# A new order of the front steps, one product for both groups' compressed scores, and fillers in three pauses

## The chip, the cores and the metric

The kernel runs as one program on one core of a Trainium2 chip. The metric is the device time of one execution in microseconds. Every number below comes from timed runs or from one profiled execution of the kernel before.

## The reference

One decoder layer over 256 tokens of width 1024, float32 throughout:

```
p = rms_norm(h) @ w_in                      # 3 parts: NSA queries/keys/values, RWKV-7 inputs, gates
o_nsa:  per 2 groups x 4 heads (64 wide): compressed attention over 15 blocks
        k_cmp = rms_norm(silu(blocks(kc) @ ck_w1) @ ck_w2), v_cmp alike without the norm
        + selected-block attention + window attention, each a masked softmax with an ALiBi slope,
        summed with three sigmoid gates
o_rwkv: RWKV-7 over 8 heads of 64: a state of 64x64 per head, group norm, bonus, gate
h = h + concat(o_nsa, o_rwkv) @ w_out
h = h + cross_attention(rms_norm(h), rms_norm(mem))      # 4 heads of 256, 256 memory tokens
h = h + moe(rms_norm(h))                    # top 4 of 32 experts, clamped SwiGLU, 1024 -> 2048 -> 1024
```

With 256 tokens there are at most four selection blocks, so all of them are taken and the selected part is plain causal attention.

## The kernel before

The kernel has two halves. The **front** computes everything up to the router. The **expert loop** then goes over "items", one expert (or the overflow of one) with up to 64 tokens each, and reads 12.6 MB of weights for each item through a ring of six 2 MB pieces in SBUF (`ring`, loaded at L2088). SyncE's queue reloads a piece as soon as TensorE signals `piece_used` for it. The first halves of items 10 to 15 are loaded ahead (L2104) into buffers that the front no longer needs. Item 0's six pieces are loaded during the end of the front, from the moment `rwkv_out` is complete, because the ring's memory serves as the front's scratch until then.

**Order of the front.** After the input projections (TensorE until about 104 us) the work is a list of small steps, `ORDER`. TensorE, VectorE, ScalarE and GpSimd each walk the same list in the same order and execute their own part of each step; each engine is in-order, so a step that waits holds up all that stands behind it on that engine. The steps are:

- `xk j`: key projection for cross-attention, quarter j (32 matmuls of 128x256; a float32 matmul appears as two instructions). ScalarE copies and squares it, GpSimd adds the two squares (L2020, `kx_squares`). `xkn j`: the sum over partitions (L675), `Sqrt` on ScalarE, reciprocal and two multiplies on VectorE. `xv n`: value projection (L684).
- `score u`, `turnp u`, `pv u`: one attention unit (u = 0 to 3 of token tile 0, 4 to 7 of tile 1): scores (L712), `Exp` on ScalarE, normalising on VectorE and GpSimd (L2016), transposes (L733), product with the values (L748, L753).
- `cmp`, `cmpout`, `cmpsc`, `turnc`: compressed keys and values. `cmp` (L474) needs its own weight slot, job `cmp` of the list `LATE`. `cmpout` (L482 to L492) goes TensorE, ScalarE, VectorE, TensorE, ScalarE, VectorE in turn and ends with `kcmpT`. `cmpsc` (L696) computes the compressed scores, with 64 rows of the array for each of the two groups and 15 columns each.
- `tok`, `parts`, `g3`, `inv 0..14`, `akv`, `qt`, `z`, `chunk 0..3`, `y`, `ymean`, `yvar`: the RWKV part. `inv s` (L551, 32 small products each) is a chain that inverts 64x64 triangular matrices; ScalarE copies some results out of PSUM, VectorE the others. `yvar 1` ends in `rwkv_out`.

PSUM results rotate over seven banks in the order of the list (`tile`), so a step also waits until the result seven tiles back has been taken. Behind the list stand the output projection (L773), whose first 32 of 128 instructions need only the attention part and whose rest waits for `rwkv_out`; the cross-attention with its own list `CROSS` (L822 to L860); its output projection with the router (L325, L874 to L914); and `gather` (L922), which collects the tokens of the first items.

**ScalarE's function tables.** The function of an ACTIVATE must be in the table set that is loaded. A set is loaded by name with `preload_act_table_set`; where none is named, the compiler places a load in front of the ACTIVATE that needs one. The code names the set that holds both `Ln` and `Exp` (`LOGEXP`) at L1623, L1666 and last in `cmpout` (L1710); from there to L1889 no set is named. Every inverse root in that stretch is the pair

```
link(f(dst, src, ACT.Ln, scale=scale, bias=...))
link(f(dst, dst, ACT.Exp, scale=-0.5), name)
```

which is used in `cmpout`, `yvar 0` and `yvar 1`, `token_rs` (twice) and the four `norm` steps of `CROSS`; `xkn` uses `ACT.Sqrt`.

**Item 0.** `hidden_bias` (L944) adds the first-layer bias as a small product; item 0 does two of them, then 32 instructions of `hidden` (L964) over the pieces 0 and 1, then the other half. VectorE's `hot` column selects the bias.

`keep_busy(n)` issues n products of 128x128 whose result nobody reads.

Of the kernel before, what the change touches and what calls it, by code (L numbers as in the profile page):

```python
# [53 lines left out]
LATE = [('xk_w', 0), ('xk_w', 1), ('xk_w', 2), ('xk_w', 3), ('xv_w', 0), ('cmp', 0), ('xv_w', 1), ('xv_w', 2),  # L54
# [41 lines left out]
def build(nc, a, out):  # L96

    ctx = ExitStack()
    with ctx:
# [32 lines left out]
        kcmpT = sb("kcmpT", 16)  # L132
# [136 lines left out]
        def matrix(q, tt, p):  # L269
# [4 lines left out]
        ORDER = [('xk', 0), ('score', 0), ('tok', 0), ('cmpin',), ('xkn', 0), ('xk', 1), ('score', 1), ('parts', 0),  # L274
                 ('xkn', 1), ('xk', 2), ('parts', 1), ('g3',), ('xkn', 2), ('xk', 3), ('xkn', 3), ('inv', 0),
                 ('inv', 1), ('xv', 0), ('inv', 2), ('cmp',), ('cmpout',), ('tok', 3), ('cmpsc',), ('inv', 3),
                 ('turnc', 0), ('xv', 1), ('turnp', 0), ('turnp', 1), ('score', 2), ('akv',), ('inv', 4), ('inv', 5),
                 ('pv', 0), ('score', 3), ('inv', 6), ('inv', 7), ('xv', 2), ('pv', 1), ('turnp', 2), ('score', 4),
                 ('inv', 8), ('xv', 3), ('turnp', 3), ('pv', 2), ('inv', 9), ('inv', 10), ('score', 5), ('tok', 1),
                 ('pv', 3), ('inv', 11), ('xv', 4), ('inv', 12), ('turnc', 1), ('turnp', 4), ('turnp', 5),  # L280
                 ('inv', 13), ('pv', 4), ('score', 6), ('inv', 14), ('score', 7), ('tok', 2), ('pv', 5), ('qt',),
                 ('z',), ('turnp', 6), ('turnp', 7), ('chunk', 0), ('pv', 6), ('chunk', 1), ('y', 0), ('pv', 7),
                 ('chunk', 2), ('xv', 5), ('chunk', 3), ('ymean', 0), ('y', 1), ('yvar', 0), ('xv', 6), ('ymean', 1),
                 ('xv', 7), ('yvar', 1)]

        CROSS = [('project', 0), ('project', 1), ('norm', 0), ('score', 0), ('score', 1), ('norm', 1),
                 ('project', 2), ('turn', 0), ('turn', 1), ('score', 2), ('score', 3), ('norm', 2), ('project', 3),
                 ('score', 4), ('score', 5), ('pv', 0), ('turn', 2), ('turn', 3), ('turn', 4), ('norm', 3),
# [14 lines left out]
        def _(pe):  # L303
# [174 lines left out]
            def cmpout_step():  # L478
                pe.wait_ge(sem("cmp_hidden"), 1)
# [177 lines left out]
            def yvar_step(tt):  # L657
                pe.wait_ge(sem("y_squared"), tt + 1)
                t = tile("yvar", tt, freed=("y_rs", tt + 1))
                pe.matmul(t, blk64[:, :], SQ, start=True, stop=True).then_inc(sem("tile_ready"), 1)  # L660
# [27 lines left out]
            def cmpsc_step():  # L688
                pe.wait_ge(sem("queries_normed"), 2)
                pe.wait_ge(sem("kcmp"), 1)  # L690
                for tt in range(TT):
                    both = [tile("cmpsc", tt, g, freed=("cmp_scores", 2 * tt + g + 1)) for g in range(NSA_G)]
                    for i in range(4):
                        for g in range(NSA_G):
                            r = slice(64 * g, 64 * g + 64)
                            mm = pe.matmul(both[g][:, i * 16:i * 16 + NCMP], qT[r, i, tt * P:(tt + 1) * P],  # L696
                                           kcmpT[r, 0:NCMP], start=True, stop=True)
                            if i == 3:
                                mm.then_inc(sem("tile_ready"), 1)
# [147 lines left out]
            def xturn(n):  # L847
                pe.wait_ge(sem("xprobs"), n + 1)
# [92 lines left out]
            def hidden_bias(g):  # L941

                n, half, r = g // 2, g % 2, slice(NE * g, NE * g + NE)
                pe.matmul(psum[64 * half:64 * half + 64, 4 + n, :], hot[r, :], bias1[r, :], start=True, stop=False)  # L944
# [1292 lines left out]
```

## Time and profile before

| | us |
|---|---|
| median of 3 runs | 1283.32 (1283.27 to 1283.56) |
| the profiled execution's own time | 1287.24 |
| its span in the profile | 1285.5 |
| TensorE busy | 1228.3 |
| TensorE weight loads busy | 620.0 |
| VectorE busy | 361.1 |
| ScalarE busy | 195.4 |
| GpSimd busy | 58.7 |
| bytes moved | 442.61 MB, mean 344 GB/s |

Busy time is an average over stages with different limits; the stages have to be read apart. In the profile L12 is line 12 of the kernel, PE is TensorE, PEld its weight load, DVE VectorE, ACT ScalarE, POOL GpSimd, and SP the queue of SyncE that issues the weight loads. All of ScalarE's activations carry the line of the helper (L1607).

### The profile page before, as it was taken

What the parts mean: (1) busy time and instruction counts of PE and PEld (TensorE: products, weight loads), DVE (VectorE), ACT (ScalarE), POOL (GpSimd) and SP (SyncE); (2) the same over time, 40 slices, a digit from 0 to 9 for tenths busy, and PEclk for the clock granted to TensorE, in tenths of its full rate; (3) what the DMA queues carried; (4) which work ended last, traced back from release to release, by engine and by line L of the source; (5) the groups of instructions that cost most, each with busy time, mean ns of one, the idle gap of its engine ahead of it and who ended that gap; (6) DMA issues with size and microseconds to landing.
All of it is one profiled execution on the core that took longest, in us unless ns stands there. A gap on an engine that the chain in (4) does not pass through costs nothing.

```text
span 1285.5 us, 19154 instructions
## 1 busy us (share of the span) xinstructions
PE 1228.3 (96%) x7762; PEld 620.0 (48%) x7762; DVE 361.1 (28%) x850; ACT 195.4 (15%) x437; POOL 58.7 (5%) x110
## 2 busy tenths in 40 slices
PE   9999898999999999999899999999999998989898
PEld 8887777788773343323234333434423232323332
DVE  4467754322235221212122121212212121212111
ACT  2333335312210000000000000000000000000001
POOL 6210001100010000000000000000000000000000
PEclk9999989999999999999999999999999999999999
DMA  7342110197379999999999999999999999999997
GB/s 261 136 150 104 67 68 35 36 369 317 122 316 400 428 428 428 429 429 428 429 427 429 421 395 424 428 428 428 428 429 429 429 428 429 428 429 428 429 427 303
DMA packets 36343, 442.61 MB, mean 344 GB/s; under 512 B 4032, under 2 KB 4160, under 8 KB 6592
## 3 DMA queue, kind: packets, MB, share of 16 engines
q1 hardware_dynamic: 35424, 440.24, 82.0%
q10 hardware_dynamic: 864, 1.57, 0.4%
q8 instruction: 43, 0.70, 0.2%
q14 instruction: 12, 0.10, 0.0%
HBM read 440.75 MB, written 1.05 MB: 344 GB/s over the span
## 4 chain that ended last, share of the span: by engine, by line
PE 63%; DMA 30%; DVE 3%; ACT 2%; issue 1%; POOL 0%; ACTq 0%; SPq 0%; DVEq 0%
DMA sb_ring<-in_mlp_w 29%; PE ps L964 23%; PE ps L993 9%; PE ps L325 8%; PE ps L922 3%; PE ps L932 2%; PE ps L822 2%; PE ps L773 2%; PE ps L684 2%; PE ps L944 1%; PE ps L551 1%; PE ps L979 1%; PE ps L338 1%; ACT sb_qx L1607 1%; PE ps L426 1%
## 5 line engine op out<-in xcount | busy, mean ns | idle before, releaser
L964 PE MATMUL ps<-sb_ring,sb_xv 128*64 128x512 f32 x1960 | 439.7, 596 | 29.7 <-DMA sb_ring<-in_mlp_w 28.7
L964 PEld LDWEIGHTS ps<-sb_ring,sb_xv 128*64 128x64 f32 x1960 | 133.5, 137 | 311.8 <-issue 252.3
L993 PE MATMUL ps<-sb_ring,sb_xv 128*64 128x512 f32 x1024 | 228.6, 596 | 0.0
L1567 DVE TENSOR_SCALAR sb_early<-ps 128x256 f32<-128x256 f32 x64 | 27.2, 425 | 646.9 <-PE ps L964 646.9
L993 PEld LDWEIGHTS ps<-sb_ring,sb_xv 128*64 128x64 f32 x1024 | 71.7, 137 | 133.1 <-issue 131.0
L1607 ACT ACTIVATE sb_early<-sb_early 128x256 f32<-128x256 f32 (+2 forms) x69 | 28.2, 409 | 512.8 <-DVE sb_early L1567 507.7
L1607 ACT ACTIVATE sb_early<-ps 128x512 f32<-128x512 f32 (+2 forms) x39 | 21.1, 543 | 280.2 <-PE ps L993 266.0
L932 PE MATMUL ps<-sb_early 64*128 64x512 f32 x248 | 61.6, 615 | 0.0
L922 PE MATMUL ps<-sb_early,sb_hnT 128*128 128x128 f32 x512 | 59.8, 275 | 0.0
L922 PEld LDWEIGHTS ps<-sb_early,sb_hnT 128*128 128x128 f32 x512 | 58.4, 192 | 0.0
L325 PE MATMUL ps<-sb_hnT,sb_wsl 128*128 128x256 f32 x256 | 56.1, 379 | 0.0
L325 PEld LDWEIGHTS ps<-sb_hnT,sb_wsl 128*128 128x128 f32 x256 | 48.6, 190 | 7.1 <-issue 0.5
L1542 DVE TENSOR_TENSOR sb_xv<-ps,sb_xv 128x512 f32<-128x512 f32 x32 | 22.1, 691 | 55.1 <-PE ps L922 55.1
L979 PEld LDWEIGHTS ps<-sb_ident,sb_xv 128*128 128x128 f32 x128 | 12.9, 141 | 50.9 <-issue 26.0
L944 PE MATMUL ps<-sb_early,sb_hot 32*64 32x512 f32 x256 | 35.9, 613 | 0.0
L1607 ACT ACTIVATE sb_xv<-ps 128x256 f32<-128x256 f32 x64 | 24.0, 375 | 50.0 <-PE ps L979 50.0
L932 PEld LDWEIGHTS ps<-sb_early 64*128 64x128 f32 x248 | 21.3, 186 | 19.8 <-issue 19.8
L684 PE MATMUL ps<-sb_wsl,sb_ox 128*128 128x256 f32 x128 | 30.8, 395 | 0.0
L325 PE MATMUL ps<-sb_qx,sb_wsl 128*128 128x256 f32 x128 | 28.4, 381 | 0.7 <-ACT sb_qx L1607 0.7
L325 PE MATMUL ps<-sb_ox,sb_wsl 128*128 128x256 f32 x128 | 28.4, 380 | 0.7 <-DVE sb_qx L1111 0.7
L979 PE MATMUL ps<-sb_ident,sb_xv 128*128 128x128 f32 x128 | 28.1, 301 | 0.5 <-DVE sb_xv L1574 0.5
L822 PE MATMUL ps<-sb_hnT,sb_wsl 128*128 128x256 f32 x128 | 28.5, 381 | 0.0
(374 smaller groups left out, 1043.1 us busy)
## 6 DMA issues: line engine op xcount, KB each, us to landing
sb_ring<-in_mlp_w SPq DMA_DIRECT2D x183, 2048.0 KB, 20.7
sb_wsl<-in_w_front SPq DMA_DIRECT2D x31, 1024.0 KB, 4.8
sb_ring<-in_mlp_w SPq DMA_DIRECT2D x5, 1024.0 KB, 21.7
sb_wsl<-in_mlp_w SPq DMA_DIRECT2D x3, 1024.0 KB, 8.9
sb_spare<-in_mlp_w SPq DMA_DIRECT2D x2, 1024.0 KB, 9.6
sb_ring<-in_mlp_w SPq DMA_DIRECT2D x4, 512.0 KB, 13.8
sb_wsl<-in_w_values SPq DMA_DIRECT2D x1, 1120.0 KB, 5.0
sb_wsl<-in_w_front ACTq DMA_DIRECT2D x4, 256.0 KB, 7.3
```

Source lines behind the costliest of these rows:

```text
L325: mm = pe.matmul(t[:, g * T:(g + 1) * T], w[:, k, g * P:(g + 1) * P], act[:, k, :], start=k == 0, stop=k == KD - 1)
L684: mm = pe.matmul(t[:, 0:T], memT[:, k, tt * P:(tt + 1) * P], wjob(J_XV[j])[:, k, :], start=k == 0, stop=k == KD - 1)
L773: mm = pe.matmul(t[:, g * T:(g + 1) * T], w[:, k, g * P:(g + 1) * P], mixT[:, k, :], start=k == 0 and g == 0, stop=k == KD - 1, skip_group ...
L822: mm = pe.matmul(t[:, g * T:(g + 1) * T], w[:, k, g * P:(g + 1) * P], hnT[:, k, :], start=k == 0, stop=k == KD - 1)
L922: mm = pe.matmul(psum[:, 4 + k // 4, k % 4 * PAIR:(k % 4 + 1) * PAIR], h[:, tt, k * P:(k + 1) * P], sel[:, tt, :], start=tt == 0, stop=tt ...
L932: mm = pe.matmul(psum[:, 2 * tt + o2, :], selgT[par][r, tt, :], yb[r, :], start=False, stop=False, skip_group_check=True)
L944: pe.matmul(psum[64 * half:64 * half + 64, 4 + n, :], hot[r, :], bias1[r, :], start=True, stop=False)
L964: mm = pe.matmul(psum[64 * half:64 * half + 64, 4 + n, :], xgT[:, k, SLOTS * par:SLOTS * par + SLOTS], w[:, at + 512 * half:at + 512 * hal ...
L979: mm = pe.transpose(psum[:, 6, m * P:(m + 1) * P], actv[:, m * P:(m + 1) * P], ident[:, :])
L993: mm = pe.matmul(psum[64 * o2:64 * o2 + 64, 7, :], actT[:, 2 * n + m, 64 * q:64 * q + 64], ring[:, at + 512 * o2:at + 512 * o2 + 512], sta ...
L1567: dve.tensor_scalar(gl, psum[:, 4 + n, 0:256], 7.0, None, ALU.min).then_inc(sem("glu"), 1)
L1607: return act.activation(o, x, func, **kw)
```

## The change

The edits: a new `ORDER`; a new `CROSS`; job `cmp` one place earlier in `LATE`; the compressed scores of both groups in one product of 128 rows by 32 columns, from a `kcmpT` that holds each group in its own rows and zeros elsewhere (eight products instead of sixteen, one PSUM tile and one VectorE add for each token tile instead of two); fillers of four products in `cmpout`, in `yvar 1` and ahead of the first `turn` of `CROSS`; the addition of the two squares in `xk` on VectorE instead of GpSimd; one small memset more on GpSimd; and item 0's bias products behind the weights' products of each half instead of ahead of them.

```
@@ -51,7 +51,7 @@
-LATE = [('xk_w', 0), ('xk_w', 1), ('xk_w', 2), ('xk_w', 3), ('xv_w', 0), ('cmp', 0), ('xv_w', 1), ('xv_w', 2),
+LATE = [('xk_w', 0), ('xk_w', 1), ('xk_w', 2), ('xk_w', 3), ('cmp', 0), ('xv_w', 0), ('xv_w', 1), ('xv_w', 2),
@@ -129,7 +129,7 @@
-        kcmpT = sb("kcmpT", 16)
+        kcmpT = sb("kcmpT", NSA_G, 16)
@@ -271,21 +271,21 @@
-        ORDER = [('xk', 0), ('score', 0), ('tok', 0), ('cmpin',), ('xkn', 0), ('xk', 1), ('score', 1), ('parts', 0),
-                 ('xkn', 1), ('xk', 2), ('parts', 1), ('g3',), ('xkn', 2), ('xk', 3), ('xkn', 3), ('inv', 0),
-                 ('inv', 1), ('xv', 0), ('inv', 2), ('cmp',), ('cmpout',), ('tok', 3), ('cmpsc',), ('inv', 3),
-                 ('turnc', 0), ('xv', 1), ('turnp', 0), ('turnp', 1), ('score', 2), ('akv',), ('inv', 4), ('inv', 5),
-                 ('pv', 0), ('score', 3), ('inv', 6), ('inv', 7), ('xv', 2), ('pv', 1), ('turnp', 2), ('score', 4),
-                 ('inv', 8), ('xv', 3), ('turnp', 3), ('pv', 2), ('inv', 9), ('inv', 10), ('score', 5), ('tok', 1),
-                 ('pv', 3), ('inv', 11), ('xv', 4), ('inv', 12), ('turnc', 1), ('turnp', 4), ('turnp', 5),
-                 ('inv', 13), ('pv', 4), ('score', 6), ('inv', 14), ('score', 7), ('tok', 2), ('pv', 5), ('qt',),
-                 ('z',), ('turnp', 6), ('turnp', 7), ('chunk', 0), ('pv', 6), ('chunk', 1), ('y', 0), ('pv', 7),
-                 ('chunk', 2), ('xv', 5), ('chunk', 3), ('ymean', 0), ('y', 1), ('yvar', 0), ('xv', 6), ('ymean', 1),
-                 ('xv', 7), ('yvar', 1)]
+        ORDER = [('xk', 0), ('tok', 0), ('score', 0), ('cmpin',), ('xkn', 0), ('xk', 1), ('score', 1), ('parts', 0),
+                 ('xkn', 1), ('xk', 2), ('parts', 1), ('g3',), ('xkn', 2), ('xk', 3), ('inv', 0), ('cmp',),
+                 ('cmpout',), ('inv', 1), ('tok', 3), ('cmpsc',), ('xkn', 3), ('xv', 0), ('inv', 2), ('akv',),
+                 ('xv', 1), ('xv', 2), ('turnc', 0), ('inv', 3), ('turnp', 0), ('turnp', 1), ('score', 2),
+                 ('inv', 4), ('pv', 0), ('pv', 1), ('inv', 5), ('score', 3), ('inv', 6), ('xv', 3), ('inv', 7),
+                 ('turnp', 2), ('inv', 8), ('turnp', 3), ('score', 4), ('score', 5), ('inv', 9), ('xv', 4),
+                 ('pv', 2), ('inv', 10), ('tok', 1), ('pv', 3), ('inv', 11), ('turnc', 1), ('turnp', 4),
+                 ('turnp', 5), ('pv', 4), ('score', 6), ('inv', 12), ('inv', 13), ('tok', 2), ('pv', 5), ('inv', 14),
+                 ('score', 7), ('xv', 5), ('z',), ('turnp', 6), ('turnp', 7), ('qt',), ('chunk', 0), ('chunk', 1),
+                 ('pv', 6), ('chunk', 2), ('y', 0), ('chunk', 3), ('pv', 7), ('ymean', 0), ('y', 1), ('yvar', 0),
+                 ('xv', 6), ('ymean', 1), ('xv', 7), ('yvar', 1)]
...
-                 ('project', 2), ('turn', 0), ('turn', 1), ('score', 2), ('score', 3), ('norm', 2), ('project', 3),
-                 ('score', 4), ('score', 5), ('pv', 0), ('turn', 2), ('turn', 3), ('turn', 4), ('norm', 3),
+                 ('project', 2), ('score', 2), ('score', 3), ('turn', 0), ('turn', 1), ('turn', 2), ('turn', 3),
+                 ('norm', 2), ('score', 4), ('project', 3), ('pv', 0), ('turn', 4), ('norm', 3), ('score', 5),
@@ -476,6 +476,7 @@
             def cmpout_step():
+                keep_busy(4)
@@ -655,6 +656,8 @@
             def yvar_step(tt):
+                if tt:
+                    keep_busy(4)
@@ -687,16 +690,13 @@
             def cmpsc_step():
...
-                pe.wait_ge(sem("kcmp"), 1)
+                pe.wait_ge(sem("kcmp"), NSA_G)
...
-                    both = [tile("cmpsc", tt, g, freed=("cmp_scores", 2 * tt + g + 1)) for g in range(NSA_G)]
+                    t = tile("cmpsc", tt, freed=("cmp_scores", tt + 1))
...
-                        for g in range(NSA_G):
-                            r = slice(64 * g, 64 * g + 64)
-                            mm = pe.matmul(both[g][:, i * 16:i * 16 + NCMP], qT[r, i, tt * P:(tt + 1) * P],
-                                           kcmpT[r, 0:NCMP], start=True, stop=True)
-                            if i == 3:
-                                mm.then_inc(sem("tile_ready"), 1)
+                        mm = pe.matmul(t[:, i * 32:i * 32 + 32], qT[:, i, tt * P:(tt + 1) * P],
+                                       kcmpT[:, :, :].rearrange("p g c -> p (g c)"), start=True, stop=True)
+                    mm.then_inc(sem("tile_ready"), 1)
...
             def score_step(u):
@@ -845,6 +845,8 @@
             def xturn(n):
+                if n == 0:
+                    keep_busy(4)
@@ -938,10 +940,11 @@
-            def hidden_bias(g):
+            def hidden_bias(g, last=False):
...
-                pe.matmul(psum[64 * half:64 * half + 64, 4 + n, :], hot[r, :], bias1[r, :], start=True, stop=False)
+                return pe.matmul(psum[64 * half:64 * half + 64, 4 + n, :], hot[r, :], bias1[r, :],
+                                 start=not last, stop=last)
...
             def hidden(i, par, n, stage, ahead, last):
@@ -963,7 +966,12 @@
-                                       w[:, at + 512 * half:at + 512 * half + 512], start=False, stop=k == KD - 1)
+                                       w[:, at + 512 * half:at + 512 * half + 512],
+                                       start=stage == 0 and k == 0, stop=stage > 0 and k == KD - 1)
+                    if stage == 0 and k == KD - 1:
+                        pe.wait_ge(sem("hot"), 1)
+                        for g in (2 * n, 2 * n + 1):
+                            mm = hidden_bias(g, last=True)
@@ -1001,10 +1009,11 @@
-                pe.wait_ge(sem("hot"), i + 1)
...
-                for g in range(2 if first else 4):
-                    hidden_bias(g)
+                if not first:
+                    pe.wait_ge(sem("hot"), i + 1)
+                    for g in range(4):
+                        hidden_bias(g)
@@ -1019,9 +1028,6 @@
-                if first:
-                    for g in range(2, 4):
-                        hidden_bias(g)
@@ -1246,8 +1252,11 @@
-                link(stt(kcmpT[:, 0:NCMP], psum[:, b, 0:NCMP], vec("k_cmp_norm_g"), crs[:, 0:NCMP],
-                         ALU.mult, ALU.mult), "kcmp")
+                dve.wait_ge(sem("kcmp_cleared"), 1)
+                for g in range(NSA_G):
+                    r = slice(64 * g, 64 * g + 64)
+                    link(stt(kcmpT[r, g, 0:NCMP], psum[r, b, 0:NCMP], vec("k_cmp_norm_g")[r, :], crs[r, 0:NCMP],
+                             ALU.mult, ALU.mult), "kcmp")
...
             def parts_step(tt):
@@ -1353,11 +1362,10 @@
-                    for g in range(NSA_G):
-                        b = ready(dve, "cmpsc", tt, g)
-                        part = sc_c[:, tt, 4 * g:4 * g + 4, 0:NCMP]
-                        link(dve.tensor_tensor(part, view(psum[:, b, :], 0, 4, 16)[:, :, 0:NCMP], part, ALU.add),
-                             "cmp_scores")
+                    b = ready(dve, "cmpsc", tt)
+                    scores = psum[:, b, 0:128].rearrange("p (j g c) -> p g j c", j=4, g=NSA_G)[:, :, :, 0:NCMP]
+                    part = sc_c[:, tt, :, :].rearrange("p (g j) c -> p g j c", g=NSA_G)[:, :, :, 0:NCMP]
+                    link(dve.tensor_tensor(part, scores, part, ALU.add), "cmp_scores")
@@ -1368,6 +1376,10 @@
+
+            def xk_step(j):
+                dve.wait_ge(sem("kx_squared"), j + 1)
+                link(dve.tensor_tensor(xsq[:, 0, :], xsq[:, 0, :], xsq[:, 1, :], ALU.add), "kx_squares")
...
             def score_step(u):
@@ -1395,8 +1407,8 @@
-                     "ymean": ymean_step, "yvar": yvar_step, "xkn": xkn_step, "cmpsc": cmpsc_step, "score": score_step,
-                     "turnp": turnp_step}
+                     "ymean": ymean_step, "yvar": yvar_step, "xk": xk_step, "xkn": xkn_step, "cmpsc": cmpsc_step,
+                     "score": score_step, "turnp": turnp_step}
@@ -1980,6 +1992,7 @@
+            link(pool.memset(kcmpT[:, :, :], 0.0), "kcmp_cleared")
@@ -2015,15 +2028,9 @@
-            def xk_step(j):
-                pool.wait_ge(sem("kx_squared"), j + 1)
-                pool.tensor_tensor(xsq[:, 0, :], xsq[:, 0, :], xsq[:, 1, :], ALU.add).then_inc(sem("kx_squares"), 1)
-
...
-                if step == "xk":
-                    xk_step(*args)
...
             def add_squares(which):
...
```

## Rows read from the trace of the kernel before

**Rows 1.** The page's slices: GB/s in 40 slices of 32.1 us.
```profile
GB/s 261 136 150 104 67 68 35 36 369 317 122 316 400 428 428 428 429 429 428 429 427 429 421 395 424 428 428 428 428 429 429 429 428 429 428 429 428 429 427 303
```
**Rows 2.** Windows: bounds, length, PE, PEld, DVE, ACT, POOL busy, PEclk, DMA share, GB/s.
```profile
100.00:262.00 162.00, 145.57 (x2358) 122.00 (x2357) 89.53 (x171) 69.38 (x162) 15.01 (x12) 0.94 0.19 65
...
388.00:390.00 2.00, 2.00 (x12) 0.73 (x13) 1.86 (x6) 0.80 (x2) 0.00 (x0) 1.00 0.90 254
...
430.00:440.00 10.00, 10.00 (x52) 3.12 (x50) 0.39 (x2) 0.60 (x1) 0.00 (x0) 1.00 1.00 425
```
**Rows 3.** Timeline of TensorE, 104 to 262 us: start, length, instructions, [idle before, releaser].
```profile
112.41 0.72 PE L712 MATMUL ps<-sb_hn 64*128 64x128 f32 x8 [0.81 <-issue]
...
145.43 0.96 PE L675 MATMUL ps<-sb_early 128*128 128x256 f32 x2 [2.37 <-POOL sb_early L2020]
...
157.96 0.29 PE L482 MATMUL ps<-sb_h1T,sb_smalls 64*64 64x15 f32 x4 [1.55 <-DVE sb_h1T L1243]
...
161.07 3.60 PE L696 MATMUL ps<-sb_kcmpT,sb_hn 64*128 64x15 f32 x32 [0.47 <-issue]
...
167.00 4.93 PE L684 MATMUL ps<-sb_wsl,sb_ox 128*128 128x256 f32 x16
...
179.36 1.16 PE L551 MATMUL ps<-sb_spare,sb_ring 64*64 64x64 f32 x45 [2.63 <-issue]
...
185.29 3.72 PE L684 MATMUL ps<-sb_wsl,sb_ox 128*128 128x256 f32 x16
...
209.81 1.38 PE L551 MATMUL ps<-sb_early,sb_spare 64*64 64x64 f32 x64 [2.14 <-ACT sb_spare L1607]
...
224.55 1.16 PE L566 MATMUL ps<-sb_ring 64*64 64x64 f32 x64 [2.04 <-ACT sb_ring L1607]
```
**Rows 4.** Windows in which the clock was low (columns as in Rows 2).
```profile
160.00:170.00 10.00, 9.54 (x109) 8.44 (x108) 6.16 (x25) 3.95 (x10) 0.50 (x1) 0.52 0.01 2
...
212.00:214.00 2.00, 2.00 (x12) 2.00 (x11) 0.00 (x0) 1.87 (x4) 0.00 (x0) 0.50 0.03 8
```
**Rows 5.** Timeline of POOL: the sum of squares of `xk 0`.
```profile
113.09 0.73 POOL L2020 TENSOR_TENSOR sb_early<-sb_early 128x256 f32<-128x256 f32 x1 [44.88 <-ACT sb_early L1607]
```
**Rows 6.** Timeline of DVE: what stands ahead of it, and a 128x256 addition.
```profile
112.34 1.42 DVE L1220 TENSOR_TENSOR sb_ring<-ps,sb_ring 128x512 f32<-128x512 f32 x2
...
236.46 0.42 DVE L1308 TENSOR_TENSOR sb_ring<-ps,sb_ring 128x256 f32<-128x256 f32 x1 [1.30 <-PE ps L622]
```
**Rows 7.** Groups by line, ACT: automatic table loads (busy, mean ns, idle before).
```profile
L1607 ACT ACT_TABLE_LOAD x4 | 5.1, 1283 | 6.7 <-DVE sb_st L1384 6.6
```
**Rows 8.** Timeline of ACT: a table load, and the pair of `yvar 0`.
```profile
120.28 1.28 ACT L1607 ACT_TABLE_LOAD   x1
121.57 0.47 ACT L1607 ACTIVATE sb_early<-ps,sb_eps_col 128x256 f32<-128x256 f32 x1
...
250.90 0.69 ACT L1607 ACTIVATE sb_ring<-ps,sb_eps_col 128x512 f32<-128x512 f32 x1 [0.46 <-PE ps L660]
251.62 0.63 ACT L1607 ACTIVATE sb_ring<-sb_ring 128x512 f32<-128x512 f32 x1
```
**Rows 9.** Timeline of DVE in `ymean 1`.
```profile
256.06 0.69 DVE L1322 TENSOR_TENSOR sb_ring<-sb_ring,ps 128x512 f32<-128x512 f32 x1
```
**Rows 10.** Timelines of PE and SP: output projection, and first ring load.
```profile
259.26 27.79 PE L773 MATMUL ps<-sb_mixT,sb_wsl 128*128 128x256 f32 x128
...
264.68 0.33 SPq L2088 DMA_DIRECT2D sb_ring<-in_mlp_w  x1
```
**Rows 11.** Timeline of PE in the cross-attention: its longest waits.
```profile
313.19 0.44 PE L851 MATMUL ps<-sb_ident,sb_hn 128*128 128x128 f32 x2 [1.44 <-DVE sb_hn L1434]
...
338.02 14.08 PE L325 MATMUL ps<-sb_qx,sb_wsl 128*128 128x256 f32 x64 [0.75 <-ACT sb_qx L1607]
```
**Rows 12.** Timelines of DVE and PE: router, and item 0's bias.
```profile
371.67 0.54 DVE L1111 SCALAR_TENSOR_TENSOR sb_early<-ps,sb_st,sb_smalls 128x32 f32<-128x32 f32 x2 [3.45 <-ACT sb_st L1607]
...
379.83 1.07 PE L944 MATMUL ps<-sb_early,sb_hot 32*64 32x512 f32 x4
```

## The prediction

> **What bounds the kernel now.** I read the slices first, then windows, then the timeline of each stage. From the middle of the trace on, the slices stand at 421 to 429 GB/s almost without a break [rows 1], and a window inside the expert loop has the DMA engines busy for 1.00 of it [rows 2]. So the second part is bound by the weight stream: 12.6 MB an item, about 29 us, while TensorE has slack there. The stream runs from the moment item 0 gives its first pieces back. The front before it isn't bound by DMA: it moves little [rows 1], and TensorE's queue is the chain. So a microsecond won or lost before `gather` is one won or lost at the end, and one inside the loop is worth nothing. The changed steps lie between 104 and 380 us.
>
> In the list (100 to 262 us) TensorE is busy for 145.57 of 162 us, so 16.4 us are idle, at a mean granted clock of 0.94 [rows 2]. That mean means 0.06 x 162 = 9.7 us of full-speed time not granted; some of it fell into idle time, so I take 8.5 as what work was stretched by. The idle time is in a few holes: 0.81, 2.37, 1.55, 0.47, 2.63, 2.14 and 2.04 us are the main ones [rows 3]. The low level (0.50 in a window, 1.2 GHz) shows soon after several of the holes [rows 4]; the same value projection takes 4.93 us at 167 us and 3.72 at 185 [rows 3]. The hole of 2.04 us wasn't followed by a fall.
>
> **The list, step by step.** I walked the new order with the durations of the old rows, each engine in order, and noted where TensorE waits.
> - Gone: the idle time but 0.5 us that lies ahead of the list, 15.9, and the 8.5 of the clock. `xkn 3` with its wait of 2.37 now stands behind `cmpsc`, when its operand is long ready; `tok 0` covers the 0.81.
> - `cmpsc`: 32 instructions took 3.60 us at half clock [rows 3, 4], 112 ns each, 56 at full; 16 fewer are worth 0.9. VectorE loses two small adds, no one waits for them. The second small write of `kcmpT` costs VectorE 0.2 and the memset is early on GpSimd, whose queue has nothing due: nothing.
> - The square sum: 0.73 us on GpSimd [rows 5] becomes about 0.42 on VectorE [rows 6]. But in `xk 0` VectorE still has the two bonus products until 113.8 [rows 6] and then a memset, so `xkn 0` can start at 114.7, while TensorE arrives at 113.2: a new hole of 1.5. Behind the waiting VectorE stand the score steps; later ones lose under 0.5 each, bounds 0 and 1.5.
> - `cmpout` comes right behind `inv 0` and `cmp`. ScalarE has the inversion's two copies and its table load (1.28) ahead of the exponential, so the wait is about 2.4 instead of 1.55: filler 1.1 and 1.3 idle. So the filler itself costs no time here.
> - `turnp 0` and `1` wait for VectorE and GpSimd: 0.95. `inv 8` 0.75, `turnp 5` 0.85, `turnp 7` 0.45, the chunk steps 2.0 together.
> - `inv 14` needs copies that on ScalarE stand behind the exponentials of `score 6`: 1.7.
> - Together 1.5 + 2.4 + 0.95 + 0.75 + 0.85 + 0.45 + 2.0 + 1.7 = 10.6 of new waits.
> - The hole of 2.63 with no releaser [rows 3] lies in a burst of weights: TensorE had nothing to issue. The new order puts slow value projections into most bursts, but not all; bounds 0 and 2.6, I take 1.3. The clock may still fall after one or two holes: bounds 0 and 8.5 (as before), I take 2.0.
> Sum: -15.9 - 8.5 - 0.9 + 10.6 + 1.3 + 2.0 = -11.4, with -17 and -4 as ends.
> `LATE` moves one load ahead of another; both slots are free over 10 us before their use: nothing.
>
> **What the list takes with it: tables.** Before, all of `xkn` (`Sqrt`) came ahead of `cmpout`, which names the set with `Ln` and `Exp`; from there on no load stands in the trace until the loop. Now `xkn 3` comes behind `cmpout`. It brings in the set of `Sqrt`, `score 2` another for `Exp`, and no one names the joint set again. An automatic load for `Exp` need not bring `Ln`. I take it that it doesn't: then each `Ln`, `Exp` pair behind it costs two loads: two in `yvar 0`, two in `yvar 1`, two in each `token_rs`, two in each of four `norm`, so 18 with the two of `xkn 3` and `score 2`. A load takes 1.283 us [rows 7], and the activation behind it follows at once [rows 8]: 2.57 a pair.
> - `yvar`: the pair's 2.57 moves y_rs from 252.3 to 254.8, VectorE's steps behind it, the subtraction of `ymean 1` (256.06 [rows 9]) and so the square that `yvar 1` waits for. TensorE starts the output projection 1.8 later than its work allows (the filler of 1.1 lies in that wait). The second pair delays `rwkv_out`, which let the ring loads go at 264.68 [rows 10], by another 2.57, and the first 32 of 128 instructions cover 7.0 us [rows 10]: 1.0 more. Together +2.8; bounds 1.1 (the filler alone) and 5.1 (both pairs bare). The ring loads wait with it; their weights are due 5 us and more later, so that is hidden.
> - `CROSS`: the wait of 1.44 at the first `turn` [rows 11] gets two scores ahead of it. But the norms' pairs hold ScalarE and, in order behind them, VectorE's copy of project 2 and later scores. I get a wait of 2.0 at `turn 0` (1.1 of it filler), 0.4 at `norm 3` and 2.0 at `turn 5`, against 1.44 + 0.64 + 0.2 before: `xout`, at 338.02 [rows 11], moves by +1.8; bounds -1.0 (nothing added) and +6.
> - Router: VectorE waits 3.45 us and starts at 371.67 on ScalarE's inverse root [rows 12]. All that follows (choice, places, selection, `gather`) hangs on it: +2.5; bounds 0 and 2.6. TensorE then idles 2.5 us ahead of `gather`; the clock may fall there: +1.4, bounds 0 and 4.8 (the ten microseconds at 160 had a mean clock of 0.52 [rows 4]).
>
> The row shows 1.28 us for a load and 0.01 until the next activation [rows 8]. The Trainium skill, ScalarE: Activation LUTs, section What ACT_TABLE_LOAD costs, has a drain of 1.38 us beside the load, 2.66 us a switch. By that rule the pairs would cost 5.3 each. The trace disagrees: ScalarE's load at 120.28 ends at 121.56 and its `Sqrt` starts at 121.57. The same page (section Table sets) says that `Ln` then `Exp` needs one load when the joint set is used, which is what the first rival is about.
>
> **Item 0's bias.** Two products of 1.07 us together move from ahead of `hidden` to behind it [rows 12]. The first quarter of piece 0 comes free 1.07 earlier, but piece 1 is given back behind the bias, at the same time as before, and the stream was already starved just then (254 GB/s at 388 [rows 2]). So 0; bounds -1.1 and 0.
>
> **Sum.** -11.4 + 2.8 + 1.8 + 2.5 + 1.4 = -2.9 us. Made against the profiled execution, 1287.24 us (span 1285.5, 1.7 around it), this is 1284.3 there; that execution is 3.9 above the median, and the difference carries over: 1283.32 - 2.9 = 1280.4.
>
> **Rivals.**
> - *The tables don't come*, since the automatic load brings the joint set. Then -11.4, +1.1 for the filler in `yvar 1` (no wait there for it to fill), -1.0 in `CROSS`: -11.3, 1272.0. For it: four automatic loads in the trace are all we see, and none was followed by an `Ln`. Against: the code names the joint set by hand each time. 5 in 100.
> - *The clock stays low.* Place: from `cmp` to `turnc`, with few columns a product, and in the same way after later holes. If thin products rather than holes bring the fall, the 8.5 us aren't won, and a filler of 1.1 changes nothing. -2.9 + 8.5 - 2.0 = +3.6: 1286.9. It decides the sign once over 5 of the 8.5 stay. For it: from 160 to 170 us TensorE was busy nearly all the time at 0.52 [rows 4]. Against: the holes ahead of each fall. 20 in 100.
> - *My walk is too dark*: half of the new waits aren't there, and no fall: -2.9 - 5.3 - 1.3 = -9.5: 1273.8. 15 in 100.
> - *A switch costs more than its row*: 1.38 more for each of some nine loads on the path, +12.4: 1292.8. This is the rule of the skill's page named above. 3 in 100.
>
> **How the numbers follow.** The forecast has 57 in 100, with its own range 1276.5 to 1284.5. A difference under 0.2% (2.6 us) can't be told from none. The forecast lies just beyond that: 27 faster, 22 same, 8 slower. With the rivals: faster 27 + 5 + 15 = 47; same 22 + 6 = 28; slower 8 + 14 + 3 = 25. The range 1273.5 to 1287.5 takes in the low clock and the lighter walk and leaves out the tables' absence and the dearer switch.
>
> **What would show it.** ScalarE's table loads 28 instead of 10, with a pair of them around every `Ln`; `cmpsc` in 16 instructions at about 1 us; the window 100 to 250 at a clock above 0.97; the output projection starting near 250 us instead of 259.26 and waiting once for `rwkv_out`; `xout` 6 to 7 us earlier than 338; VectorE's router step waiting about 6 us instead of 3.45. Wrong would be: no load behind `score 2`; a clock still at 0.94; or TensorE waits in the list over 15 us.

## The result, and the profile after

The changed kernel took 1291.01 us (median of 12 runs, 1285.31 to 1293.86), the kernel before 1283.64 beside it (12 runs, 1282.79 to 1285.08): ratio 1.0053, 95% interval 1.0043 to 1.0064. The forecast was 1280.4, faster, range 1273.5 to 1287.5: wrong in sign, and the time lies outside the range. Executions of one kernel differ by several microseconds here, so below a kernel stands for its ratio, and 0.001 is 1.3 us.

The profiled execution of after has a span of 1289.8 us, against 1285.5. The tables came as forecast. The groups of ScalarE by line, after (columns as in [rows 7]):
```profile
L1619 ACT ACT_TABLE_LOAD x22 | 28.2, 1283 | 9.5 <-DVE sb_st L1396 6.6
```
22 automatic loads instead of 4, 28 in all instead of 10. ScalarE's timeline in `yvar 0`:
```profile
244.55 1.28 ACT L1619 ACT_TABLE_LOAD   x1 [0.44 <-PE ps L663]
245.84 0.69 ACT L1619 ACTIVATE sb_ring<-ps,sb_eps_col 128x512 f32<-128x512 f32 x1
246.54 1.28 ACT L1619 ACT_TABLE_LOAD   x1
247.84 0.63 ACT L1619 ACTIVATE sb_ring<-sb_ring 128x512 f32<-128x512 f32 x1
```
Each `Ln` and each `Exp` gets its own load, with 0.01 us between load and activation, as in [rows 8]: the dearer switch of the last rival isn't there. Against this, the Trainium skill, ScalarE: Activation LUTs, section Table sets, counts one load for `Ln` then `Exp`: that holds here only after the joint set was named by hand.

The waits of the walk came too. TensorE's timeline, after:
```profile
148.03 0.29 PE L483 MATMUL ps<-sb_h1T,sb_smalls 64*64 64x15 f32 x4 [1.29 <-DVE sb_h1T L1249]
...
152.71 1.87 PE L697 MATMUL ps<-sb_kcmpT,sb_hn 128*128 128x32 f32 x16
...
210.19 1.70 PE L552 MATMUL ps<-sb_ring 64*64 64x64 f32 x64 [2.17 <-ACT sb_ring L1619]
...
227.05 0.30 PE L622 MATMUL ps<-sb_ring 64*64 64x64 f32 x2 [0.70 <-DVE sb_ring L1311]
...
254.70 7.07 PE L773 MATMUL ps<-sb_mixT,sb_wsl 128*128 128x256 f32 x32
262.70 3.50 PE L773 MATMUL ps<-sb_mixT,sb_wsl 128*128 128x256 f32 x15 [0.93 <-DVE sb_mixT L1343]
...
312.09 1.61 PE L853 MATMUL ps<-sb_ident,sb_hn 128*128 128x128 f32 x6 [1.10 <-DVE sb_hn L1446]
...
332.00 1.63 PE L853 MATMUL ps<-sb_ident,sb_hn 128*128 128x128 f32 x6 [2.10 <-DVE sb_hn L1446]
333.45 5.33 PE L862 MATMUL ps<-sb_hn,sb_vx 128*128 128x256 f32 x16
...
339.53 2.64 PE L325 MATMUL ps<-sb_qx,sb_wsl 128*128 128x256 f32 x11 [0.75 <-ACT sb_qx L1619]
...
377.77 0.66 PE L911 MATMUL ps<-sb_early,sb_before 128*128 128x64 f32 x2 [2.63 <-DVE sb_early L1480]
...
381.32 5.33 PE L924 MATMUL ps<-sb_early,sb_hnT 128*128 128x128 f32 x32
```
Forecast 1.3 idle at `cmpout` and 2.0, 2.0 in `CROSS`; here 1.29, 1.10 behind a filler of 1.05, and 2.10. `rwkv_out` is waited for once (0.93). At the router (timeline of VectorE, after) the forecast was "about 6":
```profile
375.74 0.54 DVE L1117 SCALAR_TENSOR_TENSOR sb_early<-ps,sb_st,sb_smalls 128x32 f32<-128x32 f32 x2 [6.01 <-ACT sb_st L1619]
```

What didn't come is the clock. Below, a hole is idle time of TensorE in its stream of work, and a fall is a stretch in which the granted clock stands at 0.50 (1.2 GHz). Windows, after (columns as in [rows 2]):
```profile
100.00:262.00 162.00, 149.66 (x2375) 125.94 (x2374) 95.54 (x179) 77.07 (x168) 11.73 (x8) 0.95 0.21 73
...
150.00:152.00 2.00, 2.00 (x49) 1.88 (x42) 1.13 (x3) 0.65 (x3) 0.00 (x0) 0.50 0.06 16
210.00:214.00 4.00, 3.81 (x73) 2.87 (x74) 0.00 (x0) 2.53 (x5) 0.00 (x0) 0.57 0.01 4
227.00:237.00 10.00, 9.26 (x167) 8.59 (x170) 2.90 (x7) 0.00 (x0) 0.00 (x0) 0.53 0.01 2
333.00:337.00 4.00, 3.85 (x12) 3.12 (x12) 1.18 (x7) 1.09 (x3) 0.00 (x0) 0.57 0.01 2
377.00:381.00 4.00, 3.23 (x15) 3.23 (x16) 2.82 (x15) 2.62 (x4) 0.00 (x0) 0.61 0.25 104
381.00:385.00 4.00, 4.00 (x22) 4.00 (x22) 1.43 (x9) 0.00 (x0) 0.00 (x0) 0.54 0.00 0
```
0.95 in the list, against 0.94 [rows 2]; and the clock now falls in `CROSS` and at `gather`, where before it stood at 1.00. The last 16 instructions of `CROSS` take 5.33 us there. In e1_joint, the run below without the added loads, they take 3.72 (TensorE's timeline):
```profile
327.84 3.72 PE L862 MATMUL ps<-sb_hn,sb_vx 128*128 128x256 f32 x16
```
By two-microsecond windows, the full-speed time not granted (length times 1 - PEclk) is 10.2 us up to 264 and none up to 400 in the profile of before; after 8.5 and 5.1. Of the signs that the prediction named, three failed: a clock above 0.97, an output projection near 250 us, and an `xout` 6 to 7 us earlier (it is 1.5 later).

The way through the front by starts of the same products, in us:

| | before | after | e1_joint | h1_best_fill |
|---|---|---|---|---|
| output projection | 259.26 | 254.70 | 253.29 | 248.58 |
| first product of `CROSS`'s queries | 286.89 | 283.52 | 280.92 | 276.20 |
| `xout` | 338.02 | 339.53 | 332.31 | 327.59 |
| `gather` | 376.17 | 381.32 | 370.04 | 365.32 |
| first expert product | 380.84 | 386.58 | 373.80 | 369.09 |
| span | 1285.5 | 1289.8 | 1278.2 | 1273.4 |

### The profile page after: what moved, and what is told of

Same layout as the page of the kernel before. It is cut to its first block, busy times and chain, and to the rows that moved or that the text cites. A ratio compares the mean times of both kernels' runs of the same rounds, so it can differ in the third digit from the quotient of the medians.

```text
span 1289.8 us, 19188 instructions
## 1 busy us (share of the span) xinstructions
PE 1234.1 (96%) x7770; PEld 626.2 (49%) x7770; DVE 364.9 (28%) x853; ACT 218.5 (17%) x455; POOL 55.3 (4%) x107
## 3 DMA queue, kind: packets, MB, share of 16 engines
HBM read 440.75 MB, written 1.05 MB: 343 GB/s over the span
## 4 chain that ended last, share of the span: by engine, by line
PE 45%; DMA 27%; DVE 1%; ACT 1%; issue 0%; SPq 0%; ACTq 0%; DVEq 0%
DMA sb_ring<-in_mlp_w 27%; PE ps L967 24%; PE ps L1001 10%; PE ps L924 3%; PE ps L934 3%; PE ps L325 2%; PE ps L946 1%; PE ps L987 1%; PE ps L1021 1%; PE ps L862 0%; ACT L1619 0%; PE ps L1072 0%; PE ps L876 0%; PE ps L349 0%; DVE sb_early L1117 0%
## 5 line engine op out<-in xcount | busy, mean ns | idle before, releaser
L325 PE MATMUL ps<-sb_hnT,sb_wsl 128*128 128x256 f32 x256 | 56.1, 379 | 0.0
L773 PE MATMUL ps<-sb_mixT,sb_wsl 128*128 128x256 f32 x128 | 28.1, 380 | 0.9 <-DVE sb_mixT L1343 0.9
```

Of the source, the lines that this page charges most:

```text
L325: mm = pe.matmul(t[:, g * T:(g + 1) * T], w[:, k, g * P:(g + 1) * P], act[:, k, :], start=k == 0, stop=k == KD - 1)
L773: mm = pe.matmul(t[:, g * T:(g + 1) * T], w[:, k, g * P:(g + 1) * P], mixT[:, k, :], start=k == 0 and g == 0, stop=k == KD - 1, skip_group ...
```

## The experiments

The theories: (A) the loss is the table loads, and one load of the joint set by hand removes them; (B) what the order gains is less than the sum said, because idle holes and with them the clock's falls stay.

**e1_joint**: one line in the kernel after.
```
 def xkn_step(j):    # ScalarE
     ...
     root(xrs[:, :], psum[:, b, 0:T], "kx_rs")
+    if j == 3:
+        act.preload_act_table_set(LOGEXP)
```


> The changed kernel with one line more: ScalarE names the set that holds Ln and Exp again right behind the Sqrt of xkn 3. Table theory: the 16 later loads go (28 become 12), and with them 1.7 to 2.8 us before the output projection, 3 us in CROSS, 2.5 us of wait at the router and the clock fall behind that wait (1.7), so about 9 us less than the changed kernel: near 1282 us, gather near 372 us in the trace. Rival, the clock in the list is all of it and the loads are hidden: no change, 1291 us, gather near 381.

1279.27 us (7 runs), ratio 0.9958 (0.9944 to 0.9973). Against after, 0.0095 or 12.2 us: theory A holds. Of the 18 added loads one automatic load and the one by hand are left (ScalarE's groups by line, e1_joint):
```profile
L1619 ACT ACT_TABLE_LOAD x5 | 6.4, 1283 | 5.3 <-DVE sb_st L1396 5.2
```
The loads cost more than the 8.4 of my terms: 1.7 in the list (2.8 less the filler's 1.1, which the change pays without loads too), 1.8 + 1.0 in `CROSS`, 3.9 at the router. The change without them gains 5.4, not the 11.3 of the first rival.

**e2_before_lost**: the reverse, in the kernel before.
```
 def cmpout_step():  # ScalarE, at its end
+    act.preload_act_table_set("sqrt_and_others")
```


> The kernel before, with nothing but the joint set lost: behind cmpout ScalarE names the set of Sqrt, so that each Ln, Exp pair later brings its two loads, in the old order and without fillers. Table theory: the loads alone make the kernel before 7 to 9 us slower, 1291 to 1293 us, with the router's choice waiting 6 us instead of 3.45 and a fall of the clock ahead of gather. Rival, the new order's clock and waits are what costs: under 2 us slower, 1284 to 1285.5 us.

1300.62 us (4 runs), ratio 1.0118 (1.0101 to 1.0136). ScalarE's group by line, e2_before_lost:
```profile
L1607 ACT ACT_TABLE_LOAD x21 | 26.9, 1283 | 9.8 <-DVE sb_st L1384 6.6
```
That is 21 automatic loads instead of 4 and one more by hand, 28 in all as in after. The loads alone slow the old order by 15 us, about twice the 7 to 9 expected; the new one isn't needed for it. Its profile has the two falls of after, in `CROSS` and ahead of `gather`; the rest of the excess is open.

**e3_joint_oldcross** and **e4_joint_oldbias**: e1_joint with one more part undone in each.
```
-CROSS = [...]   # order of after, filler at turn 0
+CROSS = [...]   # order of before, no filler
```


> As e1_joint, with the old CROSS list and without the filler ahead of its first turn. If the new CROSS is worth the 1.0 us that I gave it without loads, this is 1 us above e1_joint (1283). Rival: the two lists are alike within 0.5 us once no load stands in them.

0.9958 (0.9944 to 0.9972), 12 runs: without loads the new `CROSS` order is worth nothing measurable; from its first product to `xout` it takes 51.39 us in e1_joint, 51.13 before, and 52.77 in this run, with a fall behind its holes. My -1.0 for it failed.
```
 for g in ...:
-    hidden_bias(g, last=True)   # behind the products
+    hidden_bias(g)              # ahead of them
```


> As e1_joint, with item 0's bias products ahead of the weights' products as before. My account: piece 1 comes free at the same time either way, so no difference (0 to 0.5 us). Rival: the first ring load starts 1.07 us earlier with the new place, and all behind it: this one 1.1 us above e1_joint.

0.9971 (0.9958 to 0.9984), 11 runs, 1280.6: 1.3 above e1_joint, with overlapping intervals. The forecast for the new place was 0, with -1.1 as a bound; which of them holds stays open.

**f1_joint_nofill**: e1_joint without the three fillers.
```
-keep_busy(4)        # in cmpout
-if tt:
-    keep_busy(4)    # in yvar 1
-if n == 0:
-    keep_busy(4)    # at CROSS's first turn
```


> e1_joint without the three fillers of the change (cmpout, yvar 1, first turn of CROSS). If the fillers only sit in waits, the time stays at 1279.3 us; by my account the one in yvar 1 has no wait behind it once the loads are gone and the one in CROSS is longer than its wait, so this is up to 1.5 us faster. Rival, the fillers hold the clock: the low stretches in the list grow from 5 to 8.5 us of lost full-speed time toward 10, and the time goes up by 2 us or more.

0.9958 (0.9946 to 0.9970), 6 runs: the change's fillers neither cost nor bring anything measurable in time. The full-speed time not granted is 9.8 us in the mean of these runs against 7.7 in e1_joint; with 6 and 7 runs that may be chance.

**f2_joint_poolxk**: e1_joint with the square sum on GpSimd.
```
-dve.tensor_tensor(xsq[:, 0, :], xsq[:, 0, :], xsq[:, 1, :], ALU.add)
+pool.tensor_tensor(xsq[:, 0, :], xsq[:, 0, :], xsq[:, 1, :], ALU.add)
```


> e1_joint with the addition of the two squares on GpSimd again. My account: the hole of 1.5 us ahead of xkn 0 (VectorE is still at the bonus products) goes, the other three additions are as early on either engine: 0.8 to 1.5 us less, 1278. Rival: VectorE's faster addition pays at the later three steps, and this is not faster.

0.9949 (0.9933 to 0.9966), 8 runs. TensorE's wait for `xkn 0` is 0.75 instead of the 1.54 of after; the gain of 1.2 is no more than the interval.

**f3_after_routerfill**: the kernel after, loads left in, the router's hole filled.
```
-keep_busy(6)
+keep_busy(16)
```


> The changed kernel, loads and all, with ten more filler products in the router's wait (16 instead of 6 ahead of the wait for the choice), so that TensorE isn't idle for 2.6 us there. If the idle time is what brings the clock down ahead of gather, gather takes 3.7 instead of 5.3 us and the small products ahead of it half, 3 us less in all: 1288. Rival, the fall comes from something else: gather still at 5.3 us, 1291.

1.0032 (1.0020 to 1.0045), 5 runs, 1289.58. TensorE's timeline there:
```profile
380.80 0.43 PE L911 MATMUL ps<-sb_early,sb_before 128*128 128x64 f32 x2 [0.40 <-DVE sb_early L1480]
...
382.84 3.84 PE L924 MATMUL ps<-sb_early,sb_hnT 128*128 128x128 f32 x32
```
The wait for VectorE stays, the hole in TensorE's work goes (2.63 to 0.40), and `gather` runs at full clock: 3.84 us instead of 5.33. So the fall hung on the hole. In time it is 0.0021 or 2.7 us less than after, near the 3 expected, though the intervals touch.

**f4_joint_fills**: e1_joint with fillers in holes that are left.
```
-keep_busy(4)        # cmpout
+keep_busy(9)
+keep_busy(8, both[0][:, 0:P])       # inv 14, ahead of its wait
+keep_busy(2, t[:, 256:256 + P])     # each chunk, ahead of its wait
```


> e1_joint with more fillers: nine products instead of four in cmpout, eight ahead of the wait of inv 14, two in each chunk step's wait. If idle holes bring the clock down, the list keeps the full clock (loss under 2 us instead of 5 to 8.5) and the time falls by 3 us or more, to 1276, with the runs closer together. Rival, thin products of 64 rows bring it down: the falls stay and the time is 1279 to 1281.

0.9948 (0.9935 to 0.9961), 5 runs, all within 1276.42 to 1278.61. The clock is full (windows, f4_joint_fills):
```profile
104.00:400.00 296.00, 283.86 (x3116) 226.58 (x3116) 144.96 (x328) 98.25 (x227) 21.71 (x18) 1.00 0.47 183
```
The falls are gone, as expected, though holes of up to 1.63 us are left, and 8.5 us of lost full-speed time are back. The 3 us of time are not: against e1_joint it is 0.0010 or 1.3 us, inside the intervals, and the output projection starts only 2.7 earlier (250.60).

**g1_best**: f4's fillers, f2's square sum, without the fillers of `yvar 1` and of `CROSS`.
```
-if tt:
-    keep_busy(4)    # yvar 1
-if n == 0:
-    keep_busy(4)    # CROSS's first turn
```


> The kernel after, with one load of the table that holds Ln and Exp behind the root of group 3, the square sum back on GpSimd, fillers ahead of the waits of cmpout (9), inv 14 (8) and the chunks (2 each), and without the fillers of yvar 1 and of CROSS's first turn. Theory (the rest of the list's gain is lost where TensorE stands idle and its clock then falls): no stretch below 0.9 of the clock between 104 and 400 us in the profile, mean clock about 1.00, time 1275 to 1277, at or a little below the 1276.8 and 1277.9 of the two versions that had one of the two edits. Rival (falls come by chance, whatever stands in the holes): a clock of 0.990 to 0.995 as elsewhere, time 1278 to 1280. Second rival (the two dropped fillers hid something): a new low stretch right behind yvar 1 or behind CROSS's first turn and 1.7 us more.

0.9932 (0.9918 to 0.9945), 5 runs, 1275.75. One fall is left up to 400 us, and it is where the dropped filler was (TensorE's timeline, then windows, of g1_best):
```profile
304.00 2.20 PE L854 MATMUL ps<-sb_ident,sb_hn 128*128 128x128 f32 x8 [1.37 <-DVE sb_hn L1443]
```
```profile
306.00:310.00 4.00, 4.00 (x15) 3.37 (x14) 1.07 (x5) 1.43 (x5) 0.00 (x0) 0.57 0.00 0
```

**h1_best_fill**: g1_best with that filler back.
```
+if n == 0:
+    keep_busy(4)
```


> The fastest version so far (g1_best: one hand-set load, square sum on GpSimd, fillers ahead of cmpout, inv 14 and the chunks) with the 4 filler matmuls (1.1 us) ahead of CROSS's first turn put back, where TensorE waits 1.4 us at 304 us and the clock then fell for 3.4 us. Theory (the falls start behind idle holes): no stretch at the low clock between 104 and 400 us, mean clock 0.999 or 1.000, time 1274.5 to 1275.5 against 1275.75. Rival (the fall comes all the same): a stretch at 306 to 310 us again and a clock of 0.998.

0.9934 (0.9922 to 0.9947), 1275.2 us, five runs within 0.8. The hole of 1.37 is now 0.47 behind the filler, and the clock is 1.00 from 104 to 400 us (TensorE's timeline, then the window):
```profile
304.15 0.44 PE L856 MATMUL ps<-sb_ident,sb_hn 128*128 128x128 f32 x2 [0.47 <-DVE sb_hn L1445]
```
```profile
104.00:400.00 296.00, 284.86 (x3118) 226.42 (x3118) 144.17 (x324) 98.25 (x227) 25.10 (x22) 1.00 0.48 185
```
It beats both kernels: 0.66% under before, and by the two ratios 1.2% under after. In time it can't be told from g1_best.

**g2_before_fills**: only fillers, in the kernel before.
```
+keep_busy(6)                        # cmpout
+keep_busy(8, both[0][:, 0:P])       # inv 12, and the same in qt
+keep_busy(9, t[:, 256:256 + P])     # xkn 3
```


> The kernel before with nothing but fillers in its own holes: 9 ahead of group 3's squares, 6 in cmpout, 8 ahead of the inversion step at 179 us and 8 ahead of the qt product at 210 us. Theory: the falls of the clock at 145, 159, 179 and 210 us, which cost 10.2 us of full-speed time in the profile of before, go with the holes, in part paid back since the waits behind them are then met by an engine that comes early: 1276 to 1280, so 4 to 8 us below before. Rival (the falls cost little, since TensorE at half speed is waited for by nothing that matters there): 1282 to 1285. That would say why the change's eight removed microseconds of idle time and its better clock brought less than the sum.

0.9974 (0.9964 to 0.9985), 8 runs: 3.3 us for four fillers, less than the 4 to 8 expected. The falls at 145 and 210 us are gone; one is left in the compressed scores, behind a hole of 1.00 without a filler, and one behind the hole with no releaser, where no filler was tried either. A third is new, in `CROSS` from 310.7 to 314.1, behind holes that brought none in before (TensorE's timeline, then windows):
```profile
159.48 2.72 PE L704 MATMUL ps<-sb_kcmpT,sb_hn 64*128 64x15 f32 x32 [1.00 <-issue]
...
176.27 0.38 PE L556 MATMUL ps<-sb_ring 64*64 64x64 f32 x9 [2.40 <-issue]
```
```profile
160.00:168.00 8.00, 8.00 (x102) 7.20 (x102) 5.79 (x23) 2.48 (x6) 0.91 (x1) 0.57 0.01 2
177.00:181.00 4.00, 4.00 (x96) 3.37 (x91) 2.98 (x6) 1.19 (x2) 0.00 (x0) 0.57 0.03 8
```

**g3_before_cmpsc**: the merged product alone, with the writes and the memset it needs, in the kernel before.
```
-for g in range(NSA_G):   # 64 rows, 15 columns each
-    mm = pe.matmul(both[g][...], qT[r, i, ...], kcmpT[r, 0:NCMP], ...)
+mm = pe.matmul(t[:, i * 32:i * 32 + 32], qT[:, i, ...], kcmpT[...], ...)
```


> The kernel before with one part of the change alone: both groups' compressed scores in one product (16 instead of 32 matmuls, three more small VectorE results). Forecast of that term: -0.9 us. Expected 1282 to 1284, which with the clock's own spread is no difference; 1280 or less would say that the term was worth more (the 32 products ran at half speed), 1286 or more that the wait for the two cleared and written halves of the key tile costs more than the products saved.

1.0008 (0.9999 to 1.0017), 11 runs. TensorE's timeline:
```profile
159.70 3.60 PE L694 MATMUL ps<-sb_kcmpT,sb_hn 128*128 128x32 f32 x16 [0.84 <-issue]
```
16 instructions of 128 rows and 32 columns take 3.60 us at the low clock, exactly what 32 of 64 rows took [rows 3]; and the wait ahead is 0.84 instead of 0.47.

**g4_xkn3_early**: the kernel after with `xkn 3` moved, nothing preloaded.
```
-('inv', 0), ('cmp',), ... ('cmpsc',), ('xkn', 3), ('xv', 0),
+('inv', 0), ('xkn', 3), ('cmp',), ... ('cmpsc',), ('xv', 0),
```


> The kernel after with one name moved: xkn 3 ahead of cmp, so that the root of group 3 is taken before the exponential of the compressed attention and the table of the roots is not called back behind it. Nothing is preloaded. Theory (the 18 added table loads are the loss, and what sets them off is the root behind the exponential): at most 12 table loads, time 1278 to 1282, as with the preload (1279.3), less up to 2 us of TensorE's wait for group 3's squares, which then stands open earlier in the list. Rival (the loads are set off by something else, such as the yvar pairs): 28 loads or so and 1288 to 1292.

0.9985 (0.9968 to 1.0001), 7 runs, 1281.34. ScalarE's group by line, g4_xkn3_early:
```profile
L1619 ACT ACT_TABLE_LOAD x4 | 5.1, 1283 | 5.2 <-DVE sb_st L1396 5.2
```
So it is the root behind the exponential that sets the loads off. The runs lie from 1279.6 (mean clock 0.996) to 1287.87 (0.988); the profiled one is the slowest, with this (windows):
```profile
146.00:166.00 20.00, 19.57 (x182) 17.52 (x183) 13.03 (x32) 5.75 (x15) 0.00 (x0) 0.51 0.19 72
```

**h2_joint_cross** and **h3_joint_router**: the kernel after with the joint set named only ahead of `CROSS`, or only ahead of the router.
```
+act.preload_act_table_set(LOGEXP)
 block_squares("mixed")      # h2; "crossed" in h3
```


> The kernel after with one load by hand of the table that holds Ln and Exp ahead of the first block squares of CROSS: the six loads of the list stay (xkn 3, score 2, two pairs of yvar), those of CROSS and the router go. The forecast's terms for these: 2.8 for CROSS and 3.9 for the router with the clock, so 1291.0 - 6.7 = 1284.3. From the two profiles (CROSS 4.6, router 5.6, of it given back in the loop about 1.4): 1291.0 - 8.8 = 1282.2. The list's share is what is left above 1279.3.

> The kernel after with one load by hand ahead of the last block squares, behind CROSS: the loads of the list and of CROSS stay, the two of the router's inverse root go. Forecast's term: 2.5 for the wait of VectorE and 1.4 for the fall of the clock behind TensorE's idle time, so 1287.1; from the profiles (2.6 + 1.5 + what the loop gives back) 1286.9 to 1288.3. VectorE's wait there 3.45 instead of 6.0, gather 3.7 us long instead of 5.3. f3_after_routerfill, which kept the loads and filled only the hole, gave 1.4 of it.

h2 0.9979 (0.9967 to 0.9992), h3 1.0019 (1.0007 to 1.0030), 12 runs each. By differences of ratios, each uncertain by some 2 us, the loads cost 4.4 at the router (after less h3), 5.1 in `CROSS` (h3 less h2) and 2.7 in the list (h2 less e1).

## Why the prediction was wrong

| term | forecast | measured, from |
|---|---|---|
| the change, no loads | -11.3 | -5.4 (e1) |
| loads in the list | +1.7 | +2.7 (h2 - e1) |
| loads in `CROSS` | +2.8 | +5.1 (h3 - h2) |
| loads in the router, with its fall | +3.9 | +4.4 (after - h3) |
| sum | -2.9 | +6.8 |

Of the 9.7 us between the sums, 5.9 lie in the first line and 3.8 in the loads.

**The step that failed** is the clock term of the list: "the 8.5 of the clock" under "Gone", with "after one or two holes ... I take 2.0", so -6.5. What the runs showed: before has a mean clock of 0.9917 over the 80 runs beside the experiments (10.7 us of its span not granted), e1 0.9940 (7.7), after 0.9909 (11.7). The change without loads returned some 3 us, and the change as a whole none. The cause was in the prediction itself: it listed 10.6 us of new waits, holes of the same size as the old ones, and still let the falls go. In the 17 profiles I count 47 falls between 104 and 400 us; each begins in an idle hole of at least 0.6 us or within 2.5 us of its end, and these stretches are only 13% of the time. But a hole needn't bring one: of 186 such holes 136 brought none, those of 0.8 to 1.5 at 114 us never did, the hole at 145 did in before and not in g3. So one profile doesn't tell what another run of the same kernel loses. The rival "the clock stays low" (20 in 100) came near in size and had the wrong cause for the start of a fall: with more fillers in the holes (f4, h1) the same thin products ran at full clock, though holes of up to 1.6 us were left. What keeps the clock low for 10 or 20 us once it has fallen stays open.

**Size of the clock.** Over 210 runs of all these kernels, fitted within each kernel, a microsecond of full-speed time not granted goes with 0.67 us more time. By this e1's 3.0 returned are worth an estimated 2.0 where the sum had 6.5: 4.5 of the 5.9 missing in the first line. The 4.5 rest on that fit, not on an experiment. Counting waits and clock as separate terms at full price was a second flaw; I think that an engine that comes late waits less, but no run isolates it. Clock returned by fillers brought less still: g2 returned 6.4 us of clock in the mean of its runs for 3.3 of time, f4 5.7 for 1.3 against e1. The fillers take time themselves where they overrun a wait, so neither is a clean price. Even with the 4.5 the change would be 2.3 slower, since the loads cost 3.8 more than forecast.

**Merged product**: -0.9 forecast, 0.0 in duration and +1.0 (-0.1 to +2.2) in time (g3). It was costed as half the instructions at the same length each; the length doubled: 1.87 us at full clock in after, not about 1. With `CROSS`'s -1.0 that wasn't there, this is 1.9 more, 6.4 together for 5.9 missing, which is closer than the intervals can tell.

**Right**: the list's idle time (in after 12.1 us from 100 us to the output projection beside fillers of 1.16 and 1.05 in two waits; forecast 0.5 + 10.6 + 1.3 + 1.8, less 1.1 for each of the two fillers: 12.0), the 18 loads, the length of a pair, its cost in `yvar` within the interval and, in the profile, each wait it opens; the fillers at about nothing. The bias stays open.

**`CROSS`**: from its first product to `xout` +4.9 in the profile instead of +1.8. The waits are those forecast (1.05 + 1.10, 0.42, 2.10). The forecast's own waits add up to 4.4 against 2.28 before, so +2.1, not +1.8. In the profile TensorE's idle time there grows by 1.9 (5.3 against 3.4) and the filler takes 1.05; 1.6 (5.33 against 3.72) is the fall of the clock behind the last wait, which I allowed for at the router and not here; 0.3 is left.

**One to one?** The front gave back its first piece 5.7 us later (387.70 against 381.96 for the ring load), and the span grew by 4.3. So the loop took up 1.4 in this pair of profiles. But in e1_joint the load comes 7.0 earlier and the span is 7.3 shorter, in h1_best_fill 11.8 and 12.1: the 1.4 is scatter between profiles, and 1:1 stands. That TensorE has slack in the loop isn't in the rows: it shows as busy for 10.00 of 10 us beside the full stream [rows 2].

**Slips.** In the rival of the lighter walk, "no fall" is counted as 1.3, where the sum's own terms for falls are 2.0 and 1.4. The rival of the dearer switch (1292.8) lies near the measured time by luck: no drain shows. Of the 3.8 that the loads cost beyond my terms, 1.6 is the fall in `CROSS`; the rest is inside the intervals.

## What to carry to other kernels

Before reordering work across activation functions, write down which table set is active at each step: one `Sqrt` moved behind the last hand-set load of the joint set cost 12 us here, and one line got it back. Clock lost behind idle holes may be booked as won only if the holes go, and then not at full price; where new waits take their place, book none, and compare kernels by the clock of their runs as well as by their time. Fillers returned most of the clock here but little time (1.3 us in f4, 3.3 in g2), so measure them one by one. Merging two half-height products into one of full height halved the count here, not the time: look for a row of the new shape before costing it.

## What the hardware did that I had not expected

- The same program loses different amounts of clock: g4's runs at 0.988 and 0.996 differ by 8.3 us. Most stretches at the low clock are some 3.4 or 10 us long (after: 210 to 214, 227 to 237), a few 7 or 14, one 20 (g4, 146 to 166), and TensorE was busy for 19.57 of those 20 us without the clock coming back. The Trainium skill, TensorE: Matmul & The Clock Gate, Part 1, likewise reports that the number of slow products at the start of one kernel varies from run to run.
- An instruction of 128 rows by 32 columns took 225 ns at the low clock (g3), one of 64 rows by 15 took 112 [rows 3]. In after, at a clock that had just risen, 16 of the former took 1.87 us, 117 ns each.
- The clock also fell behind a hole in which TensorE has no releaser ("issue", 2.40 in g2). Whether a filler in its own queue would cover such a hole no run shows.
